# Three residual projections, their norms and the first two products of the next stage in one block each, with the scaling on ScalarE

## What is computed

```
# first block, after the two attentions
mixed = concat([o_sb, o_gla], -1) @ w_out
x  = x + (1 + gate1) * mixed
h2 = rms_norm(x, g_norm2) * (1 + scale2) + shift2
u  = causal_depthwise_conv(h2 @ w_up, w_conv, b_conv)      # then silu gate, w_down
x  = x + (1 + gate2) * (... @ w_down)
# second block, after self-attention
x  = layer_norm(x * DN_ALPHA + mixed @ w_o + b_o, ln1_g, ln1_b)
q  = x @ xa_wq + xa_bq                                      # then attention over a memory
x  = layer_norm(x * DN_ALPHA + o @ xa_wo + xa_bo, ln2_g, ln2_b)
x  = layer_norm(x * DN_ALPHA + relu(x @ w_up + b_up)**2 @ w_down + b_down, ln3_g, ln3_b)
```

## Time and profile before

| | us |
|---|---|
| median of 3 runs (3711.05 to 3712.67) | 3711.9 |
| profiled execution | 3710.77 |
| its span, first to last instruction | 3709.0 |
| TensorE busy in the span | 3118.6 (84%) |
| VectorE / ScalarE / GpSimd busy | 1785.8 / 955.5 / 965.7 |

### The profile page before, as it was taken

The page is one execution under the profiler, slowest core; times in us unless marked ns, Lnnn a source line. Parts: engine busy times, 40 slices in busy tenths (PEclk is TensorE's granted clock), DMA queues, the critical chain, the costliest instruction groups (busy, mean ns, idle before and its releaser), DMA issues. The chain is left out here.

```text
span 3709.0 us, 42139 instructions
## 1 busy us (share of the span) xinstructions
PE 3118.6 (84%) x16524; PEld 2666.7 (72%) x16524; DVE 1785.8 (48%) x2896; ACT 955.5 (26%) x1387; POOL 965.7 (26%) x336
## 2 busy tenths in 40 slices
PE   8697999676999999994758647978888699999995
PEld 6576999566788888873646536778667688888884
DVE  1411767334445555465168866873234443333335
...
GB/s 263 109 109 86 64 81 60 101 91 40 58 46 34 57 45 57 45 12 51 63 68 86 105 67 69 49 107 35 46 136 97 36 62 46 56 45 45 51 39 57
DMA packets 111991, 257.38 MB, mean 69 GB/s; under 512 B 49760, under 2 KB 71731, under 8 KB 95590
## 3 DMA queue, kind: packets, MB, share of 16 engines
...
## 5 line engine op out<-in xcount | busy, mean ns | idle before, releaser
L837 PE MATMUL psum<-h_hi,w_hl 128*128 128x512 f32 x2432 | 753.8, 391 | 6.8 <-PEq L370 4.1
L825 POOL TENSOR_TENSOR w_hl<-w_raw,w_hl 128x2048 fp32r<-128x2048 f32 x65 | 324.8, 4997 | 938.3 <-ACT w_hl L819 938.3
L837 PEld LDWEIGHTS psum<-h_hi,w_hl 128*128 128x128 f32 x2432 | 458.7, 189 | 105.1 <-issue 8.5
L850 PE MATMUL psum<-w_hl,ffn_a_hi 128*128 128x512 f32 x1600 | 498.3, 393 | 6.3 <-DVE residual L1060 6.3
L837 PE MATMUL psum<-h_lo,w_hl 128*128 128x512 f32 x1216 | 475.3, 391 | 0.0
L610 PE MATMUL psum<-w_hl,h_hi 128*128 128x256 f32 (+1 forms) x2048 | 380.7, 289 | 30.7 <-POOL w_hl L571 13.8
L610 PE MATMUL psum<-h_hi,w_hl 128*128 128x512 f32 (+1 forms) x1152 | 350.8, 389 | 49.2 <-POOL w_hl L571 23.5
L571 POOL TENSOR_TENSOR w_hl<-w_raw,w_hl 128x2048 fp32r<-128x2048 f32 (+1 forms) x39 | 177.8, 4560 | 680.2 <-ACT w_hl L563 667.1
L850 PEld LDWEIGHTS psum<-w_hl,ffn_a_hi 128*128 128x128 f32 x1600 | 301.3, 188 | 73.0 <-DVE residual L1060 6.8
L610 PEld LDWEIGHTS psum<-w_hl,h_hi 128*128 128x128 f32 x2048 | 329.7, 198 | 32.9 <-issue 18.5
L819 ACT ACTIVATE w_hl<-w_raw 128x2048 fp32r<-128x2048 f32 x65 | 124.5, 1915 | 741.8 <-PE psum L850 357.9
...
## 6 DMA issues: line engine op xcount, KB each, us to landing
...
```

The source lines that it names most:

```text
L825: pool.tensor_tensor(self.k.w_lo[s][:, :], self.k.w_raw[s][:, :], self.k.w_hi[s][:, :].bitcast(F), ALU.subtract).then_inc(self.k.wsem["w_r ...
L837: m = pe.matmul(k.bank[b][:, :], w[:, t * CW + f * P:t * CW + (f + 1) * P], h[:, t, half * 512:half * 512 + 512], start=t == 0 and w is w_ ...
L850: m = pe.matmul(k.bank[4 + out % 4][:, :], a[:, f, tile * P:(tile + 1) * P], w[:, f * D + half * 512:f * D + half * 512 + 512], start=f == ...
```

## The change

`residual_norm` takes the place of `project_residual` and `norm`, three times; `load_rows` is gone, and the `gate2` row is loaded in `ffn_conv`, into the tile of `gate1`. Two token tiles are finished with each bank b of the last chunk ("pair b"). Statistics are taken by chunk (256 columns), so that a pair's mean and variance are there as soon as its last bank has been added. VectorE multiplies by the gain (for a layer norm it subtracts the mean in the same instruction, per pair), ScalarE multiplies by 1/std. The shift is no longer added by GpSimd to `residual`: ScalarE and VectorE add it after the transpose, where it is one number per partition (`scol`, loaded as 128 by 8 single numbers), when they write `h_hi` and `h_lo`; for layer norms the next stage's bias gets `ALPHA * shift` (`before`, one more row to load and one instruction). 16 "units" are transposed: units 0 to 7 are one block of 128 columns for tiles 0 to 3, units 8 to 11 two blocks each for tiles 4 and 5, units 12 to 15 for tiles 6 and 7. Four transposes each. The first two banks of the next stage (tokens 0 to 511) are made in the same block (`early_products`); for this the order of banks in an up product and in `xq` becomes halves of the tokens first. `first_slot=0` for two projections makes their last chunk use slot 1, with the next stage's first in slot 0.

The core of the diff (`...` marks what is left out):

```diff
+def residual_norm(k, name, lin, kind, gain, shift, hh, hl, ahead, gate=None, bias=None, before=None):
+    nc, n = k.nc, lin.n
+    units = [((0, 1, 2, 3), (t,)) for t in range(KT)] + \
+            [(tiles, (2 * j, 2 * j + 1)) for tiles in ((4, 5), (6, 7)) for j in range(4)]
+    with ExitStack() as c:
...
+        y = [k.sb(c, f"{name}_y{j}", [P, D]) for j in range(6)] if kind == "rms" else None
+        target = lambda i: k.x[:, i, :] if kind == "ln" else y[i % 6][:, :]
+        first, last = lin.s0, (n - 1) % 2 ^ lin.s0
+        assert n % 2 == 0 and ahead.first_slot == first
+        unit_bank = lambda m: k.bank[4 * (first if m < KT else last) + m % 4]
+        tokens = lambda tiles: slice(tiles[0] * P, (tiles[-1] + 1) * P)
+        part = lambda m, j: unit_bank(m)[:, j * len(units[m][0]) * P:(j + 1) * len(units[m][0]) * P]
+        with nc.Block() as block:
+            @block.sync
+            def _(sp):
+                if bias is not None:
+                    sp.dma_start(brow[:, :], rows(bias)).then_inc(bias_in, 16)
+                if before is not None:
+                    sp.dma_start(prow[:, :], rows(before)).then_inc(bias_in, 16)
+                lin.chunks(sp, lambda c, i, s: lin.load(sp, c, i, s))
+                sp.dma_start(grow[:, :], rows(gain)).then_inc(gain_in, 16)
+                sp.dma_start(scol[:, :], shift.rearrange("(t p) -> p t", p=P), allow_slow_non_contiguous=True)\
+                  .then_inc(shift_in, 16)
+                ahead.early(sp, "load", 2)
+            @block.scalar
+            def _(act):
+                lin.split_hi(act)
+                ahead.early(act, "hi", 1)
+                act.wait_ge(eps_made, 1)
+                act.wait_ge(shift_in, 16)
+                def root(b):
+                    act.wait_ge(var_done, b + 1)
+                    act.activation(std[:, 2 * b:2 * b + 2], mv[:, 2 * b:2 * b + 2, 1], ACT.Sqrt, bias=eps[:, 0:1])\
+                       .then_inc(std_done, 1)
+                def scale(b):
+                    act.wait_ge(rstd_done, b + 1)
+                    for i in (2 * b, 2 * b + 1):
+                        act.activation(target(i), target(i), ACT.Copy, scale=rstd[:, i:i + 1]).then_inc(normed, 1)
+                def upper(start, count):
+                    for m in range(start, start + count):
+                        tiles, blocks = units[m]
+                        act.wait_ge(turned, m + 1)
+                        for j, t in enumerate(blocks):
+                            a = act.activation(hh[:, t, tokens(tiles)], part(m, j), ACT.Identity, bias=scol[:, t:t + 1])
+                        a.then_inc(hi, 1)
+                root(0)
+                scale(0)
+                root(1)
+                scale(1)
+                upper(0, 4)
+                root(2)
+                scale(2)
+                upper(4, 4)
+                upper(8, 4)
+                root(3)
+                scale(3)
+                upper(12, 4)
+            @block.gpsimd
+            def _(pool):
+                pool.memset(eps[:, :], EPS if kind == "rms" else LN_EPS).then_inc(eps_made, 1)
+                lin.split_lo(pool)
+                ahead.early(pool, "lo", 1)
+            @block.tensor
+            def _(pe):
+                def turn_units(start, count):
+                    for m in range(start, start + count):
+                        tiles, blocks = units[m]
+                        pe.wait_ge(normed, tiles[-1] + 1)
+                        if m == 0:
+                            pe.wait_ge(*lin.at("lin_evac", first, lin.banks * lin.uses[first]))
+                        elif m < KT:
+                            reached(pe, lo, m - 3)
+                        elif m < KT + 4:
+                            pe.wait_ge(*lin.at("lin_evac", last, lin.banks * (lin.uses[last] - 1) + m - KT + 1))
+                        else:
+                            pe.wait_ge(lo, m - 3)
+                        for j, t in enumerate(blocks):
+                            for at, i in enumerate(tiles):
+                                mm = pe.transpose(part(m, j)[:, at * P:(at + 1) * P], target(i)[:, t * P:(t + 1) * P],
+                                                  k.ident[:, :])
+                        mm.then_inc(turned, 1)
+                def between(ch, b):
+                    if ch == n - 1 and b == 2:
+                        turn_units(0, 4)
+                lin.products(pe, between)
+                turn_units(4, 4)
+                turn_units(8, 4)
+                pe.wait_ge(lo, KT)
+                ahead.early_products(pe, hh, hl, 0)
+                turn_units(12, 4)
+                ahead.early_products(pe, hh, hl, 1)
+            @block.vector
+            def _(dve):
+                if bias is not None:
+                    dve.wait_ge(bias_in, 16 if before is None else 32)
+                    if before is not None:
+                        dve.scalar_tensor_tensor(out=brow[:, :], in0=prow[:, :], scalar=ALPHA, in1=brow[:, :],
+                                                 op0=ALU.mult, op1=ALU.add).then_inc(biased, 1)
+                        dve.wait_ge(biased, 1)
+                    scaled_residual(k, dve, brow[:, :], scaled)
+                def pair_norm(b):
+                    pair = mv[:, 2 * b:2 * b + 2, :]
+                    dve.wait_ge(added, NT * (n - 1) + 2 * b + 2)
+                    dve.bn_aggr(mv[:, 2 * b, :], st[:, 2 * b, :, :].rearrange("p c s -> p (c s)")).then_inc(aggr, 1)
+                    if kind == "ln":
+                        dve.wait_ge(aggr, b + 1)
+                    dve.bn_aggr(mv[:, 2 * b + 1, :], st[:, 2 * b + 1, :, :].rearrange("p c s -> p (c s)"))\
+                       .then_inc(aggr if kind == "rms" else var_done, 1)
+                    if kind == "rms":
+                        dve.wait_ge(aggr, 2 * b + 2)
+                        dve.tensor_tensor(std[:, 2 * b:2 * b + 2], pair[:, :, 0], pair[:, :, 0], ALU.mult)\
+                           .then_inc(squared, 1)
+                        dve.wait_ge(squared, b + 1)
+                        dve.tensor_tensor(pair[:, :, 1], pair[:, :, 1], std[:, 2 * b:2 * b + 2], ALU.add)\
+                           .then_inc(var_done, 1)
+                    else:
+                        dve.wait_ge(var_done, b + 1)
+                    for i in (2 * b, 2 * b + 1):
+                        if kind == "rms":
+                            if i >= 6:
+                                dve.wait_ge(turned, KT)
+                            e = dve.tensor_tensor(target(i), k.x[:, i, :], grow[:, :], ALU.mult)
+                        else:
+                            e = dve.scalar_tensor_tensor(out=target(i), in0=k.x[:, i, :], scalar=mv[:, i, 0:1],
+                                                         in1=grow[:, :], op0=ALU.subtract, op1=ALU.mult)
+                        e.then_inc(gained, 1)
+                    dve.wait_ge(std_done, b + 1)
+                    dve.wait_ge(gained, 2 * b + 2)
+                    dve.reciprocal(rstd[:, 2 * b:2 * b + 2], std[:, 2 * b:2 * b + 2]).then_inc(rstd_done, 1)
+                def lower(start, count):
+                    for m in range(start, start + count):
+                        tiles, blocks = units[m]
+                        dve.wait_ge(hi, m + 1)
+                        for j, t in enumerate(blocks):
+                            dst = (slice(None), t, tokens(tiles))
+                            e = dve.scalar_tensor_tensor(out=hl[dst], in0=part(m, j), scalar=scol[:, t:t + 1],
+                                                         in1=hh[dst].bitcast(F), op0=ALU.add, op1=ALU.subtract)
+                        e.then_inc(lo, 1)
+                def step(ch, i, s):
+                    if ch == n - 1:
+                        dve.wait_ge(gain_in, 16)
+                        dve.wait_ge(shift_in, 16)
+                    for b in range(4):
+                        if ch == n - 1 and b == 3:
+                            lower(0, 8)
+                        dve.wait_ge(*lin.at("lin_mm", s, 4 * i + b + 1))
+                        cols = slice(ch * CW, (ch + 1) * CW)
+                        for j in range(2):
+                            src = lin.out(s, b)[:, j * CW:(j + 1) * CW]
+                            xt = k.x[:, 2 * b + j, cols]
+                            if gate is not None:
+                                dve.tensor_tensor(tmp[:, j, :], src, gate[:, cols], ALU.mult).then_inc(gated, 1)
+                                dve.wait_ge(gated, ch * 8 + (2 * b + j + 1))
+                                src = tmp[:, j, :]
+                            e = dve.tensor_tensor(xt, xt, src, ALU.add)
+                        e.then_inc(k.wsem["lin_evac"][s], 1)
+                        dve.wait_ge(*lin.at("lin_evac", s, 4 * i + b + 1))
+                        for tile in (2 * b, 2 * b + 1):
+                            dve.bn_stats(st[:, tile, ch, :], k.x[:, tile, cols]).then_inc(added, 1)
```

(19 more changed lines are left out.)

183 lines of the change are left out of this document (107 added, 76 removed).

## The result

The changed kernel takes 3612.77 us (median of 4 runs, 3609.61 to 3615.01), the one before 3711.48 (4 runs, 3708.57 to 3712.67). The ratio is 0.9735 with a 95% interval of 0.9718 to 0.9751: faster, by 98.7 us. The prediction said 3622, with 3606 to 3645 as its range. The profiled execution has a span of 3607.7 us, 101.3 less than before.

The account below looks back on a forecast made before the run. TensorE was taken to bound the kernel, with three idle gaps around the norms as the prize: 104.2 us of stage gains, less 11.8 for the clock and 2.4 for handovers, gave 90 us and 3622, range 3606 to 3645.

Parts of the forecast that it names:

- Stage gains at the full clock: Three stretches between a residual projection and the product behind its norm: 39.5, 34.3 and 30.4 us gained, 104.2 in sum.
- The pair's 5.9 us on VectorE: First stage, last chunk: gate, add, statistics, small operations, gains and reciprocal for one pair take VectorE 5.9 us.
- the wait of 2.64: First stage: TensorE waits 2.7 us for the scaled pair 1 before the first transposes.
- the fourth bank's late addition: First stage: lows queued in front on VectorE delay the fourth bank's add by 4.1 us, and unit 11 waits for it.
- the case of switched tables: ScalarE's interleaved root, scaling and writing switch tables: 5 us a stage, gain 75, 3637 us; chance 0.04.
- The third stage's stall: Block behind the third norm: VectorE's rows, residual scaling and evacuations hold TensorE 9.7 us; sign: a wait of 8 to 11.
- The clock: TensorE's waits in all stages each may cost a stretch at the lower clock: 11.8 us charged.
- The long wait: Third stage: the lower clock behind TensorE's 9.7 us wait was charged 3.2 us.
- short waits: Lower clock behind three short TensorE waits per stage: 3.6 us charged in the first, 2.5 in each other.
- The case in which TensorE stays at the lower clock: Lower clock through all of each block's end: gain 59, 3653 us; half way 3637; chance 0.17.
- Handovers: Between engines, counted at nothing in the steps: about 0.05 us each, some 15 a stage, 2.4 us.
- The slower case: VectorE waits for the shift column's load; from 100 us for it the kernel gets slower, 3772 at 120; chance 0.03.

Follow-up runs that it names:

- e1: Against the changed kernel, VectorE in the last block evacuates and squares the first group before adding the shift row and scaling the residual, with a separate bias semaphore: 3599.5 us.
- e2: The changed kernel with VectorE's first evacuation and squares before the residual scaling, but still waiting until all three rows have landed: 3604.5 us.
- e3: Against the changed kernel, the two early products of each stage are taken out; all four banks are computed in the next stage's block: 3637.4 us.

## Why the prediction was right

*Stage gains at the full clock, 39.5, 34.3, 30.4.* Measured: 39.6 (41.5 less the 1.9 from ahead of the stage); 34.5 (77.5 us ahead where the third stage begins, 43.0 where the second does; 33.9 of it up to the third `xq` bank); 26.8 (104.3 less 77.5). The pair's 5.9 us on VectorE, the two statistics at 0.38 each, the wait of 2.64, the fourth bank's late addition and the early products are as drawn. That the first figure fits to 0.1 us is in part luck: it holds for an execution in which the clock stayed up, and three of five have 2.8 us less. The second and the third stage have one table load of 1.28 us each, with the root of the second 0.02 us behind it, so the case of switched tables (0.04) did not come.

*The third stage's stall*, 9.7, was mis-sized: it is 12.8, outside the 8 to 11 us that were given as a sign. The term was the scaling of eight tiles at 10.8 us, taken from a place where GpSimd was mostly idle: there one of the eight met the end of a split and took 2.85 us, and the others 1.2. Here the sum is 13.5, because one of the eight, 5.5 us long, meets all of GpSimd's split of 4.5; the first instruction took 1.75 in place of 1.3. e1 and e2 showed that the order of the queue, not the rows, makes the stall, and e3 that the scaling takes 9.2 where GpSimd is idle.

*The clock*, 11.8. The long wait cost what was charged, 3: TensorE returns 104.3 us ahead and the kernel ends 101.3 ahead, and in e1, where the wait is gone, the clock stays at 1.00 there. The 8.6 for short waits was too much: 2.5 for each of the second and third stages measured 0, and the first stage's 3.6 measured 0 in two traces and 2.8 in three. The case in which TensorE stays at the lower clock (0.17) did not come: with the early products between the waits the clock fell at most for some us, and only in the first stage. e3, without them, comes near to that case, at 0.50 behind waits of 2.60 and 5.69 us.

*Handovers*, 2.4: nothing of the kind is left in the difference. *Elsewhere*: 1.9 us ahead of the first stage and 1.5 between the first two (43.0 - 1.9 - 39.6), which were no part of the sum and are within what runs of one program differ by there. In all: 39.6 + 34.5 + 26.8 - 3.0 + 1.9 + 1.5 = 101.3 us between the two profiled executions, where 90 were forecast. The mechanism was right at each step that the traces show; of the sizes, the third stage's gain was 3.6 too large, and the charges of 8.6 for short waits and 2.4 for handovers were too heavy by all they held in this trace. These errors have opposite signs and in part cancel. By the medians the forecast is 9 us too high, inside its range. The slower case (the shift column's load) never neared: no engine waited for it.
